# An attention loop in which a cache unit's scores and values share a step, and state-space products one tile later

## The reference

```python
h = h + 0.5 * _swiglu(_rms(h, g_ffn1), ...)              # D_FF 2816
proj = _rms(h, g_mix) @ w_in    # -> a_in 512, c_q 384, c_kv 256, k_r 32, gates g_a, g_b 1024 each
ys, hT = _s5(a_in, h0, ...)     # diagonal complex scan over time, 32 groups x 64 states
z = gelu(ys);  y_a = (z * sigmoid(z @ w_glu + b_glu)) @ w_a_out
ckv = _rms(c_kv, g_kv); krope = rope(k_r)
q = _rms(c_q, g_q) @ w_uq       # 8 heads; rope on 32 of 96 columns; q_lat = q_nope @ w_uk
o = attention                   # prompt: causal, 512 keys; new tokens: 4096 cached rows + themselves
h = h + (sigmoid(g_a) * y_a + sigmoid(g_b) * (o @ w_uv @ w_b_out)) @ w_out
h = h + 0.5 * _swiglu(_rms(h, g_ffn2), ...)
```

## Time and profile before

| | |
|---|---|
| median of 3 runs | 1581.46 us (1580.78 to 1583.42) |
| the profiled execution, its own time | 1570.45 us |
| its span in the trace | 1568.7 us |
| PE busy | 1414.4 us, 90% of the span |
| DVE, ACT, POOL busy | 606.5, 412.5, 381.3 us |
| mean DMA rate | 121 GB/s |

### The profile page before, as it was taken

The page is one execution under the profiler, slowest core; times in us unless marked ns, Lnnn a source line. Parts: engine busy times, 40 slices in busy tenths (PEclk is TensorE's granted clock), DMA queues, the critical chain, the costliest instruction groups (busy, mean ns, idle before and its releaser), DMA issues.

```text
span 1568.7 us, 28581 instructions
## 1 busy us (share of the span) xinstructions
PE 1414.4 (90%) x11800; PEld 1280.2 (82%) x11800; DVE 606.5 (39%) x961; ACT 412.5 (26%) x662; POOL 381.3 (24%) x391
## 2 busy tenths in 40 slices
PE   6999999999988888878788878789999999999995
PEld 6999999999987774656565645478999999999994
DVE  5344244243465772323232235135542332323324
ACT  5232212222332113212222123123332222222223
POOL 3237262272214343111111111003122012022023
PEclk9999999999999988989999989789999999999997
DMA  5223222222241034666666666434222321322311
GB/s 209 79 82 96 79 69 95 80 81 82 68 155 45 12 123 147 212 209 210 221 211 212 200 222 213 162 116 161 81 81 77 98 93 61 106 86 71 108 42 69
DMA packets 77491, 189.13 MB, mean 121 GB/s; under 512 B 10065, under 2 KB 10994, under 8 KB 77074
## 3 DMA queue, kind: packets, MB, share of 16 engines
q1 hardware_dynamic: 73042, 179.13, 34.8%
q0 software_dynamic: 2048, 4.20, 1.0%
q10 hardware_dynamic: 2304, 4.46, 0.7%
HBM read 178.06 MB, written 9.69 MB: 120 GB/s over the span
## 4 chain that ended last, share of the span: by engine, by line
PE 72%; DVE 9%; DMA 7%; ACT 4%; POOL 4%; issue 3%; SPq 2%; DVEq 0%; POOLq 0%; ACTq 0%
PE d L1452 49%; PE e L1740 9%; DMA kv<-kv_src 6%; PE e L1668 3%; PE e L1687 2%; SPq L355 2%; DVE w_lo L972 2%; ACT w_hi L532 2%; PE e L1671 2%; DVE x_lo L977 1%; PE d L1708 1%; DVE rstd L982 1%; DVE h L1011 1%; PE d L1623 1%; POOL hid L799 1%
## 5 line engine op out<-in xcount | busy, mean ns | idle before, releaser
L972 DVE TENSOR_TENSOR w_lo<-raw,w_hi 128x1024 fp32r<-128x1024 f32 (+2 forms) x200 | 227.8, 1139 | 556.2 <-ACT w_hi L532 556.0
L1452 PE MATMUL d<-x_hi,w_hi 128*128 128x272 f32 x1568 | 329.4, 291 | 17.2 <-DVE w_lo L972 11.7
L1452 PE MATMUL d<-x_hi,w_lo 128*128 128x272 f32 x1568 | 326.8, 290 | 0.0
L532 ACT CAST w_hi<-raw 128x1024 fp32r<-128x1024 f32 (+2 forms) x200 | 191.3, 957 | 510.6 <-PE d L1452 452.0
L1452 PE MATMUL d<-x_lo,w_hi 128*128 128x272 f32 x1568 | 325.3, 289 | 0.0
L1452 PEld LDWEIGHTS d<-x_hi,w_hi 128*128 128x128 f32 x1568 | 249.0, 190 | 21.3 <-DVE w_lo L972 11.9
L1452 PEld LDWEIGHTS d<-x_lo,w_hi 128*128 128x128 f32 x1568 | 248.4, 190 | 0.0
L1452 PEld LDWEIGHTS d<-x_hi,w_lo 128*128 128x128 f32 x1568 | 246.9, 190 | 0.0
L799 POOL TENSOR_TENSOR hid<-silu,up 128x544 f32<-128x544 f32 x44 | 59.6, 1355 | 495.9 <-DVE up L1000 495.5
L1452 PE MATMUL d<-hid_hi,w_hi 128*128 128x272 f32 x704 | 149.2, 293 | 11.5 <-DVE h L1011 5.9
L1452 PE MATMUL d<-hid_hi,w_lo 128*128 128x272 f32 x704 | 146.2, 289 | 0.0
(11 more groups left out here) (295 smaller groups left out, 1879.6 us busy)
## 6 DMA issues: line engine op xcount, KB each, us to landing
kv<-kv_src SPq DMA_DIRECT2D x256, 256.0 KB, 3.7
raw<-w_gu SPq DMA_DIRECT2D x88, 512.0 KB, 3.4
raw<-w_post SPq DMA_DIRECT2D x34, 512.0 KB, 4.3
raw<-w_d1b SPq DMA_DIRECT2D x16, 384.0 KB, 3.2
raw<-w_d2b SPq DMA_DIRECT2D x16, 384.0 KB, 3.2
raw<-w_in SPq DMA_DIRECT2D x10, 512.0 KB, 3.5
gates<-gate_m ACTq DMA_DIRECT2D x16, 272.0 KB, 2.1
gate_m<-gates SPq DMA_DIRECT2D x16, 272.0 KB, 3.9
```

Of the source, the lines that this page charges most:

```text
L532: nc.scalar.copy(w_hi[:, s % 2, 0:n, :], raw[:, raw_pos(s), 0:n, :]).then_inc(S.hi_done, 1)
L972: nc.vector.tensor_tensor(w_lo[:, s % 2, 0:n, :], raw[:, raw_pos(s), 0:n, :], w_hi[:, s % 2, 0:n, :].bitcast(FP), ALU.subtract).then_inc(S ...
L1452: ins = mm(d[:, par, b, 0:HALF], w[:, pos, c0 + k, :], x[:, k, b * HALF:(b + 1) * HALF], start=first, stop=stop)
```

## The change

In the loop on PE, step `n` now does `unit_scores(n)`, `scores(n)`, the first job, `unit_turn(n)`, `turn(n - 1)`, `values(n - 2)`, `unit_values(n)` and the second job. The scores of unit `n` thus open the step in which its values are made, where they used to be made in the step before. DVE's `unit_max(n)` and ACT's `unit_exp(n)` move with them, `unit_max` ahead of the prompt's maximum and of `inverse_sum(n - 1)`. SP's loop is unchanged, so the pages are still asked for at the same place. The values of the prompt stay two steps behind.

In the projections `column_sums(N_Q)` goes from tile 6 to tile 7, `chunk_inputs(2)` from 7 to 8, `chunk_inputs(3)` stays at 9, but ahead of the rotated key's products and `outputs(0)`, which go behind query tile 0; `column_sums(N_KV)` and `outputs(1)` go from query tile 1 to 2, `outputs(2)` from 4 to 5. DVE, ACT and POOL follow. In the new tokens' part `keys(0)` moves between the two halves of the values, and the transposition `new_t` between the prompt's value products.

```diff
@@ -631,13 +631,12 @@
...
                                      scale=gains[:, G_Q + k:G_Q + k + 1]).then_inc(S.cqh_done, 1)
-            if i == IR:
+            if i == IK:
                 root(N_Q, 0, Q_LORA)
-            if i == IK:
-                scan_out(0)
             if i >= IK:
...
                 square(N_KV, i - IK, ckv[:, i - IK, :])
+        scan_out(0)
         split_hi(S_Q + 2, T_Q + 2)
...
@@ -704,17 +703,15 @@
...
 
-        unit_exp(0)
         for n in range(4 * H):
-            unit_turned(n)
+            unit_exp(n)
             w = (n % 4 + 1) * P
...
                                  accum_out=astat[:, 1, n:n + 1]).then_inc(S.exp_done, 1)
-            if n + 1 < UNITS:
-                unit_exp(n + 1)
+            unit_turned(n)
             if n >= 1:
...
@@ -905,8 +902,8 @@
...
         sum_in(2)
+        add_squares(N_KV, LC)
         sum_out(2)
-        add_squares(N_KV, LC)
         sum_in(3)
...
@@ -1195,19 +1192,17 @@
...
             if i == 7:
-                inverse(N_Q, rq)
                 for c in range(QC):
                     scaled_lo(cq_lo[:, c, :], cq[:, c, :], G_Q + c, cq_hi[:, c, :], S.cqh_done, c + 1, S.cq_ready)
+            if i == 8:
+                inverse(N_Q, rq)
                 forward(2)
-            if i == 8:
                 link(nc.vector.tensor_scalar(rq[:, :], rq[:, :], SCALE, None, ALU.mult))
                 link(nc.vector.tensor_tensor(trigq[:, :], trig[:, :], rq[:, :], ALU.mult))
+            if i == 9:
                 scan(2)
-            if i == 9:
-                dve.wait_ge(S.krot_done, 1)
-                nc.vector.tensor_copy(halves(krope[:, :]), e[:, 0:2, 0:HALF]).then_inc(S.krope_done, 1)
+                forward(3)
                 backward(2)
-                forward(3)
 
...
@@ -1221,14 +1216,17 @@
...
                 split_lo(S_Q + hd // 2 + 2)
+            if hd == 0:
+                dve.wait_ge(S.krot_done, 1)
+                nc.vector.tensor_copy(halves(krope[:, :]), e[:, 0:2, 0:HALF]).then_inc(S.krope_done, 1)
             if hd == 1:
                 scan(3)
-            if hd == 2:
+            if hd == 3:
                 inverse(N_KV, rkv)
...
                                                    in1=rkv[:, :], op0=ALU.mult, op1=ALU.mult).then_inc(S.kvn_done, 1)
-            if hd == 3:
+            if hd == 4:
                 backward(3)
...
@@ -1269,7 +1267,6 @@
...
         nc.vector.tensor_copy(v_new[0:NEW, :], e[0:NEW, 2, 256:256 + KV_LORA]).then_inc(S.vnew_done, 1)
-        keys(0)
         dve.wait_ge(S.new_exp, 1)
...
@@ -1278,7 +1275,8 @@
...
             nc.vector.tensor_copy(o_n[0:HT, 4 * r:4 * r + 4, :].rearrange("p (k b) n -> p k (b n)", k=2), e[0:HT, 0:2, :]).then_inc(S.new_done, 1)
-        unit_max(0)
+            if r == 0:
+                keys(0)
 
...
@@ -1331,12 +1329,11 @@
...
             now = jobs(n)
+            unit_max(n)
+            dve.wait_ge(S.s_pe, n + 1)
+            nc.vector.tensor_reduce(astat[:, 0, n:n + 1], d[:, 0, n % 2, 0:w], AX.X, ALU.max, negate=True).then_inc(S.nm_done, 1)
             if n >= 1:
                 inverse_sum(n - 1)
-            dve.wait_ge(S.s_pe, n + 1)
-            nc.vector.tensor_reduce(astat[:, 0, n:n + 1], d[:, 0, n % 2, 0:w], AX.X, ALU.max, negate=True).then_inc(S.nm_done, 1)
-            if n + 1 < UNITS:
-                unit_max(n + 1)
             for k in now[:1]:
...
@@ -1573,30 +1570,30 @@
...
                 chunk_inputs(1)
-            if i == 6:
+            if i == 7:
                 column_sums(N_Q, 0, (S.fwd_done, 2))
-            if i == 7:
+            if i == 8:
                 pe.wait_ge(S.rms_done, N_Q + 1)
                 chunk_inputs(2)
-            if i == 8:
+            if i == 9:
                 pe.wait_ge(S.fwd_done, 3)
+                chunk_inputs(3)
+
+        for hd in range(H):
+            wx = dict(wait_x=S.cq_ready, value=0) if hd == 0 else {}
+            tile(S_Q + hd // 2, T_Q + hd, (S_Q + hd // 2) % 2, 3 * (hd % 2), QC, cq_hi, cq_lo, **wx)
+            if hd == 0:
+                pe.wait_ge(S.fwd_done, UC)
                 pe.wait_ge(S.ktrig_done, 1)
...
                 outputs(0)
-            if i == 9:
-                pe.wait_ge(S.krope_done, 1)
+            if hd == 2:
+                column_sums(N_KV, 0, (S.krope_done, 1))
                 pe.wait_ge(S.y_out, 1)
-                chunk_inputs(3)
-
-        for hd in range(H):
-            wx = dict(wait_x=S.cq_ready, value=0) if hd == 0 else {}
-            tile(S_Q + hd // 2, T_Q + hd, (S_Q + hd // 2) % 2, 3 * (hd % 2), QC, cq_hi, cq_lo, **wx)
-            if hd == 1:
-                column_sums(N_KV, 0, (S.fwd_done, UC))
                 outputs(1)
-            if hd == 4:
+            if hd == 5:
                 pe.wait_ge(S.rms_done, N_KV + 1)
...
@@ -1635,20 +1632,26 @@
...
         pe.wait_ge(S.vw_in, 32)
-        for k in range(4):
+
+        def prompt_values(k):
             for c in range(LC):
...
             ins.then_inc(S.vp_pe, 1)
+
+        prompt_values(0)
+        prompt_values(1)
         pe.wait_ge(S.new_exp, 1)
...
         ins.then_inc(S.new_t, 1)
-        keys(0)
+        prompt_values(2)
+        prompt_values(3)
         pe.wait_ge(S.vnew_done, 1)
...
             if r:
+                keys(0)
                 pe.wait_ge(S.new_done, r)
...
@@ -1742,22 +1745,20 @@
...
         pe.wait_ge(S.new_done, 2)
-        unit_scores(0)
         pe.wait_ge(S.krope_cp, 1)
...
             now = jobs(n)
+            unit_scores(n)
             scores(n)
-            unit_turn(n)
-            if n + 1 < UNITS:
-                unit_scores(n + 1)
             for k in now[:1]:
                 job(k)
+            unit_turn(n)
             if n >= 1:
                 turn(n - 1)
-            unit_values(n)
             if n >= 2:
                 values(n - 2)
+            unit_values(n)
             for k in now[1:]:
...
             if i == 0 and hd + 1 < H:
```

## The result

| | before | after |
|---|---|---|
| median of 4 runs each | 1581.12 us (1575.33 to 1583.42) | 1468.05 us (1467.01 to 1470.07) |
| the profiled execution | 1570.45 us | 1467.01 us |
| its span | 1568.7 us | 1465.2 us |

The ratio is 0.9292, with a 95% interval of 0.9265 to 0.9318. The sign and the place are as forecast. From here on the loop runs from the first scores of a unit to the product behind its last step.

The account below looks back on a forecast made before the run. Neither PE nor DMA was full; PE's page waits before the unit's scores bound the loop. Terms 72.1 - 13 + 18 + 10 + 4 = 91 us took 1570.45 to 1479.4, plus 11.0 carried over: 1490 us, range 1470 to 1520.

Parts of the forecast that it names:

- The mechanism: Attention loop: a whole step more of PE work between page trigger and first use removes the page waits, +72.1 us.
- the 15 named: Attention loop: PE would instead wait at the turn or the values, by under 15 us.
- The 4 us for steps 0 to 20: Attention loop: thin cover for the copy and hops before the unit's values, charged at 0.2 us a step.
- the 5 for steps 24 to 27: Attention loop: gating work on ACT and DVE stands before the next maximum, 1.2 us lost in each step.
- the term's total: Attention loop: new waits as a unit's chain lies in one step, -13 us; bounds 0 and -74.
- the clock's term: Attention loop: part of PE's matmul time at the lower clock comes back, +18 us; bounds 0 and 41.
- the projections' term: Projections: products a tile later shorten PE's waits, and the last query tiles' clock recovers, +10 us; bounds 0 and 18.
- the carry-over of 11.0 us: Whole kernel: the median shown stood 11.0 us above the profiled execution, and this was added to the forecast.
- The transfers don't pace the loop: Rival, attention loop: transfers keep the mean rate near 225 GB/s, the loop gains 45 us; 1522 us, chance 0.18.
- The clock came back: Rival it answers, attention loop: small products hold the clock down, all terms but the 18 us; 1508 us, chance 0.16.
- the wait did not stay: Rival it answers, attention loop: scores still find no page, only projections and new tokens gain; 1567 us, chance 0.05.
- the unit's bare chain: Rival, attention loop: DVE's maximum late in every step exposes the chain, 3.6 us a unit; 1610 us, chance 0.04.

Follow-up runs that it names:

- e3: The kernel before, with the page loads behind unit 2 and the waits for them left out: 1464.76 us, ratio 0.9349.
- e15: The changed kernel with each page of the loop asked for one step later: 1636.13 us, ratio 1.0345.
- e12: The kernel before with the attention loop's edits alone, run again in the third group: 1468.03 us, ratio 0.9338.
- e17: The changed kernel unaltered, run again in the fifth group: 1470.92 us, ratio 0.9307.
- e9: The changed kernel with POOL's eight indirect rotary loads issued 59 us earlier on its queue: 1460.13 us, ratio 0.9291.
- e10: The changed kernel with rotary loads held back and the first three gates fetched as each buffer comes free: 1457.58 us, ratio 0.9265.
- e11: The changed kernel with rotary loads held back and the unit's values done ahead of the prompt's: 1460.3 us, ratio 0.929.
- e7: The changed kernel with POOL's eight rotary loads held back until the scan's last outputs are done, second group: 1456.68 us, ratio 0.9206.
- e5: The changed kernel unaltered, run again in the second group: 1467.9 us, ratio 0.9275.
- e18: The changed kernel with the rotary loads held back until the scan's last outputs are done, fifth group: 1458.4 us, ratio 0.9223.
- e4: The changed kernel, with the page loads behind unit 2 and the waits for them left out: 1452.46 us, ratio 0.9275.
- e2: The kernel before with the projections' edits alone, first group: 1558.18 us, ratio 0.9941.
- e16: The kernel before with the projections' edits alone, run again in the fifth group: 1577.12 us, ratio 0.9977.
- e1: The kernel before with the attention loop's edits alone, first group: 1469.58 us, ratio 0.9383.
- e14: The changed kernel with 64 already met waits added on PE ahead of the projections: 1471.24 us, ratio 0.9303.

## Where the prediction was right, and which of its steps failed

**The mechanism held.** The waits of the unit's scores went as forecast (72.1 us to 1.0), and no other large wait took their place: the loop was forecast at 331 us and took 310.8. The waits inside the unit's chain and for the gates and the like are all of the 11.5 us of idle time but 1.0, against 2.6 besides the pages before (74.7 - 72.1): some 8 us, where I had 13. The wait at the turn is 4.4 us and at the values 0.7, together under the 15 named. None of the turn's waits is in a step with a product of 24 matmuls, which was the sign of being wrong: they are in steps 21, 22 and 27, the three without a first product. Unit 23's pages came 0.95 us late, where I had 2 us:

```profile
838.92 0.71 PE L1683 MATMUL e<-ident,p_n 128*128 128x128 f32 x4 [0.81 <-ACT p_n L666]
845.20 0.71 PE L1683 MATMUL e<-ident,p_n 128*128 128x128 f32 x4 [0.83 <-ACT p_n L666]
848.67 1.07 PE L1671 MATMUL e<-kv,qlat 128*32 128x256 f32 x16 [0.95 <-DMA kv<-kv_src]
890.12 0.71 PE L1683 MATMUL e<-ident,p_n 128*128 128x128 f32 x4 [2.71 <-ACT p_n L666]
```

The 4 us for steps 0 to 20 were 0.7, and the 5 for steps 24 to 27 didn't come; a wait of 3.2 us for `a_part` came in step 29 instead. So the term's total was near, in part by luck. In the projections the wait for `m_sum` is 1.3 us (1 forecast), for `s_fwd` 5.2 (3.3) and for `qparts` 4.8 (1.3 + 2.2):

```profile
PE e L1604 <- issue: 5.4, 1, 5.4
PE e L1589 <- DVE s_fwd L1141: 5.2, 1, 5.2
PE d L1449 <- DVE qparts L1215: 4.8, 3, 2.3
PE e L1556 <- issue: 3.5, 9, 1.0
PE e L1540 <- ACT m_rms L549: 1.6, 1, 1.6
PE e L1463 <- POOL m_sum L786: 1.3, 1, 1.3
```

The first row, 5.4 us at the end of the query tiles, was 3.3 in my list. The price of DVE's later queue was thus put too low by about 5 us in these three rows, and the term came to 6.4 us instead of 10, within its bounds.

**The failed step in the loop is the size of the clock's term.** "I take less than half, +18 us" should have been up to 36.3. (e3, with the old order, had its busy time fall by 30.0 at the same 0.99, so some 6 of the 36.3 may be something other than the clock.) The 82 us at the lower level were worked out rightly from the earlier trace rows, and so was the bound of 41; but I took the low clock of the last eleven steps for a property of their small products. The loop with all pages and the loop without any (e3) both have 0.99 over those same products, and e15, with more waits, has 0.86. In the last 95 us of the loop alone the clock was 0.86 before, 0.82 in e15, 0.98 in the changed kernel and 1.00 in e3. So in this loop the waits for pages pulled the clock down, in the last third too. A small part stays that the waits don't explain: in the same 95 us e12 has 0.96 and e17 0.93. The Trainium skill, "TensorE: Matmul & The Clock Gate", section "HAM oscillation — how this bites in real kernels", says as much of a loop that stands for transfers, and here the traces agree (0.90 with 72.1 us of waits, 0.99 with 1.0, 0.86 with 127.5).

The Trainium skill's section "A second HAM failure mode: psum-queue depth-cycling" on that page, which I held against it, stands neither shown nor refuted: the changed loop has only eight pauses, 11.5 us in all, at 0.99, so it doesn't test frequent ones. Of the 82 us at the low level half could come back, 41 us, and nearly all of that did. Behind the loop 4.7 us more came, which I had not counted. The clock went from 0.87 to 1.00 in the first 52 us there, in which PE did 366 matmuls instead of 333. That the clock is its cause was not tested.

The range failed with this term. It was said to hold the forecast with its bounds, but the clock's own bound of 41 in the sum gives 1467, below its lower end of 1470.

**The failed step ahead of the loop** is that no rival and no term held the stops. With the stops the two stretches ahead of the loop bring -0.6 us instead of 14. Without them the parts are worth 8 to 10 us: in one group e12 took 1468.0, and e9, e10 and e11 took 1460.1, 1457.6 and 1460.3. That is below the 14 forecast and the 12 to 15 expected; the projections' term is the one that was too large (6.4 for 10), and the new tokens' edits are worth 6.0, against 4 (bounds 1.5 and 5). The stops ate the rest: with the loads held back the changed kernel gains 11.2 us (e7 against e5) and 12.5 (e18 against e17), of which 7.6 and 8.4 are in the stops' own stretch. "Nothing moves on POOL's queue" was true of the order, but the time at which the eight loads go out did move against PE's work: `outputs(3)` ran from 592.4 us beside loads from 589.8 on, and now from 585.5 beside loads from 583.5 on.

**The failed step around the sum is the carry-over of 11.0 us.** I took the distance between the profiled execution and the median for a property of the measurement. It belongs to this kernel's own spread: its medians run from 1567.7 to 1583.8 over the groups, and its single runs from 1561 to 1589. That its page waits are the reason is likely and not shown. The single runs of all kernels without long waits for pages stay within 5 us of their own median, and the changed kernel's median is 1.0 us above its profile.

The 22 us between forecast and result are these steps. The profiled execution came 12.4 us below the 1479.4: 22.4 in the loop (18 of it the clock), 4.7 behind it, less 14.6 ahead of it. The other 10 are the carry-over. The largest two errors, the clock and the carry-over, pointed the same way, and the stops hid a part of them: that the result lies only 2 us outside the range is luck. Without the stops (e7) the time lies 13 us below it.

**The rivals.** The transfers don't pace the loop: it moves 263 GB/s over 310.8 us, more than the 253 of the best 30 us before and the 247 that my forecast needed. They are not free, though: e4 bounds their price at 3 to 9 us, and in e10, with earlier gates, the wait for pages is 3.5 us instead of 1.0. The limit of 358 GB/s named in the prediction isn't one for this kernel over short times: from 570.8 to 573.8 us the changed kernel's transfers ran at 406 GB/s. The clock came back, the wait did not stay, and the unit's bare chain (3.6 us a step) did not appear: the waits for `p_n` and `pt_n` are 5.1 us in all, in five of 32 steps.

**The best version** is the changed kernel with the rotary loads held back: 1456.7 us (e7) and 1458.4 (e18), 11.2 and 12.5 us below the changed kernel in the same groups, and by the ratios 7.9 and 7.8% below the kernel before.

**What stays open.** In the two groups where kernels with stops and kernels with later loads stand side by side, the stops need the eight indirect loads beside `outputs(3)`: e7 and e18 have none there. e9, e10 and e11 have none either, in a group without a kernel that would show stops, and the 56 further loads in the changed kernel's loop bring none. That isn't enough: e2 and e4 had the loads beside it and no stops, e16 had them with e2's program. Nor is it shown why the kernels without the projections' edits (before, e1, e3, e12), in which loads and matmuls overlap too, have none. What PE lacks in a stop isn't in the trace. One rival is open: instructions. The changed kernel's trace has a load of 0.02 MB on an instruction queue between 584 and 586 us. But e2 and e7 have one there too, without stops, and e14's shift changed nothing, so such a load alone is not it.

## What to carry to other kernels

Where an engine waits for a transfer that a buffer's release triggers, count the work between trigger and first use, and move the use before adding buffers: here one step of slack turned 72 us of waits into 1, with the same ring and the same loads. Price the clock with the waits: here 82 us stood at the lower level, half of that is 41, and up to 36 came back with the waits; matmuls that were slow behind a wait (3.77 us against 3.21) were the sign of it. After such a gain look at what now runs side by side for the first time, and move the suspected neighbour, with an unmoved kernel measured beside it each time.

## What the runs showed of the hardware that was unexpected

- PE can stop between matmuls that wait for no semaphore the profile shows, in groups of four or five every 0.7 to 1.4 us, while POOL issues indirect loads (0.94 us each, every 1.25 us). 64 matmuls took 10 us instead of 2.07, and holding the loads back gained 11.2 and 12.5 us in all. The same program had it in one group of runs and not in another, under the same chip number (e16, e2).
- The granted clock of a stretch can differ between groups for the same program: 21.5 us busy at 0.78 in e1 and 18.5 us at 0.92 in e12, for the same products of the new tokens.
- A loop that waits for 256 KB pages varied with the group of runs by 1% (medians of 1567.7 to 1583.8 us for the kernel before), one that doesn't by 0.2% (1467.9 to 1470.9 for the changed kernel, in three groups). The cause was not tested.
- Some 82 MB of pages and weights moved at a mean of 263 GB/s beside matmuls at a clock of 0.99, and the loop was 3 to 9 us longer than without the pages (306.0 us in e4).
